# mLSTM head vectors broadcast by DMA through a small DRAM tensor; the first block's output projection computed by token halves, with its norm split the same way

## What is computed

```python
def first_block(x, c, ...):                    # the parts that matter here
    # projections: u, v, q, k, mv, o, gates ga / gb, input and forget gates
    # mLSTM branch, 4 heads of 256: running maximum m_t of the gates, then
    s   = (q @ k.T) * exp(dmat - m_t)          # weights of every (token, source) pair
    den = maximum(abs(sum(s)), exp(-m_t))      # floor of the denominator, per token and head
    h   = (s @ v) / den                        # then normed per head, gated
    x = x + gate1 * (merged @ w_out)           # the first output projection, "out1"
    y = rmsnorm(x, norm2_g) * (1 + scale2) + shift2
    x = x + ... squared_relu(y @ w_ff1) @ w_ff2
```

## Time and profile before

| | |
|---|---|
| median of 3 runs | 3258.81 us (3256.1 to 3259.67) |
| the profiled execution's own time | 3258.92 us |
| its span in the profile | 3257.2 us |
| granted PE clock, mean | 0.994 of full |
| PE busy | 3211.0 us, 99% |
| DVE / ACT / POOL busy | 57% / 16% / 7% |

### The profile page before, as it was taken

How to read it: one execution, slowest core, us unless ns; L and a number is a source line. 1 busy time by engine, 2 the same in 40 slices (tenths; PEclk the granted TensorE clock), 3 DMA queues, 4 the chain that set the end, 5 groups by cost and what they waited for, 6 DMA issues and landing times.

```text
span 3257.2 us, 35901 instructions
## 1 busy us (share of the span) xinstructions
PE 3211.0 (99%) x14194; PEld 2556.8 (78%) x14194; DVE 1849.5 (57%) x3204; ACT 514.0 (16%) x1068; POOL 226.4 (7%) x197
## 2 busy tenths in 40 slices
PE   9999999999999999999899999999999998999999
PEld 3888744888888888884478888888888744788888
DVE  6357835664337764453766664466644537766643
ACT  2111121000001000114521000110001145210001
POOL 1244400000000000003000000000000030000000
PEclk9999999999999999999999999999999999999999
DMA  5244311222222222223012222222222230122221
GB/s 235 91 172 164 117 52 45 72 91 91 88 84 91 82 86 84 97 73 123 1 52 79 90 91 81 88 91 91 84 88 88 73 123 1 53 91 79 90 81 62
DMA packets 43207, 286.16 MB, mean 88 GB/s; under 512 B 5248, under 2 KB 5248, under 8 KB 12064
## 3 DMA queue, kind: packets, MB, share of 16 engines
q1 hardware_dynamic: 39024, 271.14, 23.5%
q0 software_dynamic: 4016, 12.73, 1.2%
HBM read 279.66 MB, written 2.10 MB: 87 GB/s over the span
## 4 chain that ended last, share of the span: by engine, by line
PE 92%; DVE 5%; DVEq 1%; ACT 1%; issue 1%; DMA 0%; ACTq 0%; POOL 0%
PE ps L847 76%; PE ps L555 4%; PE ps L536 3%; PE ps L1226 2%; PE ps L1194 1%; PE ps L874 1%; DVE arena L1820 1%; PE ps L954 1%; DVE arena L2213 1%; ACT arena L1521 1%; PE ps L1208 1%; DVEq L2226 1%; PE ps L1233 0%; PE ps L1165 0%; PE ps L1158 0%
## 5 line engine op out<-in xcount | busy, mean ns | idle before, releaser
L847 PE MATMUL ps<-arena 128*128 128x256 f32 x5456 | 1245.1, 379 | 0.7 <-DVE arena L1911 0.6
L847 PEld LDWEIGHTS ps<-arena 128*128 128x128 f32 x5456 | 1036.3, 190 | 142.8 <-DVE arena L1911 1.6
L847 PE MATMUL ps<-arena,ring 128*128 128x256 f32 x2768 | 646.3, 379 | 0.5 <-ACT arena L1266 0.5
L847 PEld LDWEIGHTS ps<-arena,ring 128*128 128x128 f32 x2768 | 525.6, 190 | 72.5 <-ACT arena L1266 0.9
L847 PE MATMUL ps<-xn,ring 128*128 128x256 f32 x2272 | 520.7, 380 | 5.8 <-DVE arena L1636 2.4
L847 PEld LDWEIGHTS ps<-xn,ring 128*128 128x128 f32 x2272 | 432.3, 190 | 72.4 <-issue 9.6
L1630 DVE TENSOR_TENSOR arena<-arena,ps 128x512 f32<-128x512 f32 x169 | 116.0, 687 | 537.2 <-PE ps L847 508.1
L1606 DVE TENSOR_TENSOR arena<-ring 128x512 f32<-128x512 f32 (+1 forms) x190 | 128.3, 675 | 347.5 <-PE ps L847 347.2
L847 PE MATMUL ps<-xn,arena 128*128 128x256 f32 x1264 | 302.2, 379 | 0.0
L847 PEld LDWEIGHTS ps<-xn,arena 128*128 128x128 f32 x1264 | 240.2, 190 | 32.7
L1433 ACT ACTIVATE arena<-arena 128x512 f32<-128x512 f32 x88 | 55.5, 630 | 883.6 <-DVE arena L2091 883.5
(11 more groups left out here) (312 smaller groups left out, 2359.0 us busy)
## 6 DMA issues: line engine op xcount, KB each, us to landing
ring<-in_w_up_a SPq DMA_DIRECT2D x44, 1024.0 KB, 4.8
ring<-in_w_up_b SPq DMA_DIRECT2D x44, 1024.0 KB, 4.8
ring<-in_w_ff SPq DMA_DIRECT2D x32, 1024.0 KB, 4.8
ring<-in_w_ada SPq DMA_DIRECT2D x24, 1024.0 KB, 4.9
ring<-in_w_down_a SPq DMA_DIRECT2D x16, 1024.0 KB, 4.9
ring<-in_w_down_b SPq DMA_DIRECT2D x16, 1024.0 KB, 4.8
ring<-in_w_in SPq DMA_DIRECT2D x14, 1024.0 KB, 4.9
ring<-in_w_out SPq DMA_DIRECT2D x12, 1024.0 KB, 4.9
```

The source lines that it names most:

```text
L847: mm = nc.tensor.matmul(out_ap, w, operand(product, quads[i]), start=at not in opened, stop=last_chunk and i == len(quads) - 1, skip_group ...
```

## The change

**Head vectors.** The spread matmuls and the eight ACT copies are gone. POOL, before its weight sums of chunk 8, waits for `rows_ready` and writes rows 4 and 5 (4 partitions, 16 KB) to a DRAM tensor `cell_rows`. After its last weight sums and `pair_taken` of pair 24 (the target lies where the operands of the first products were) it issues eight transfers, each of which reads one 2 KB row for all 128 partitions (256 KB written). DVE waits for the four of `neg_m`. ACT waits for the four of `e_mt` and squares them in place, four operations of 512, ahead of its first exponentials.

**Output projection.** `out1` runs over the token halves: first 8 tiles with 256 columns into banks 0 to 3, then 8 tiles with 256 columns into banks 4 to 7. In the first half four tiles are interleaved (k 0 to 5 of all four, then k 6 and 7). A ring slot comes free only in the second half. DVE's and ACT's work on a tile has 256 columns and is done twice.

**Second norm.** Per half, one matmul of `ones` with that half of `ssq` (128 x 256) sums and spreads in one; ACT makes the inverse root with Ln and Exp on 128 x 256 into `rq`; DVE scales by `rq`. The first half's sum is issued after tile 1 of the second half, its scaling and shifts between tiles 3 to 6 of it. The second half's sum is issued after product a of `ff1` pair 0, followed by e of pair 0 and a, e of pair 1, which read the first token half only; then the rest of pair 0 (f c d b g, quad by quad), then the rest of pair 1 (g f c d b). The idle matmuls are gone. The weight sums of `ff1` 1 move from tile 6 to behind the activation sums.

```diff
-SPREADS = [(), (0, 1, 2), (3, 4, 5), (6, 7)]
@@ POOL
                 if n == 8:
                     pool.wait_ge(sem("ws_base"), GROUPS)
+                    pool.wait_ge(sem("rows_ready"), 1)
+                    nc.gpsimd.dma_start(cell_rows, rows[:, 4:6, :]).then_inc(sem("rows_out"), 16)
...
+            pool.wait_ge(sem("rows_out"), 16)
+            pool.wait_ge(sem("pair_taken"), FIRST_PAIRS)
+            for hd in range(HEADS):
+                for which, places in enumerate((neg_m, e_mt)):
+                    row = cell_rows[hd:hd + 1, which, :].to_broadcast([P, S])
+                    nc.gpsimd.dma_start(places[:, hd, :], row).then_inc(sem(f"spread_{which}"), 16)
@@ PE, spread_rows
-                for n in SPREADS[st]:
-                    hd, which = n // 2, n % 2
-                    wait(pe, "spread_read", n - 1)
-
-                    pick = consts[0:HEADS, IDENT, hd:hd + 1].to_broadcast([HEADS, P])
-                    nc.tensor.matmul(ps[:, 4 + which, :], pick, rows[:, 4 + which, :], start=True, stop=True)\
-                        .then_inc(sem("spread"), 1)
@@ PE, after the cell
-            pe_product(pe, "out1", lambda k: merged[:, k, :], 0, lambda k: (sem("merged_ready"), k + 1), None, 6)
-            wait_evacuated(pe, "out1", 5)
-            pe_norm(pe, 0, SQUARES["n2", 0] + DT)
-            pe_busy(5, 4)
+            def out1(half, places):
+
+                for t, k in places:
...
+                        elif t >= BANKS:
+                            pe.wait_ge(sem("out1_read"), DT * half + t - BANKS + 1)
+                    if half == 0 and t < BANKS:
+                        pe.wait_ge(sem("merged_ready"), k + 1)
...
+                    mm = nc.tensor.matmul(out1_bank(half, t), ring[:, slot, unit * UNIT:(unit + 1) * UNIT],
+                                          merged[:, k, side(half)], start=(k == 0), stop=(k == DT - 1))
...
+            def out1_sum(half):
+                pe.wait_ge(sem("out1_read"), DT * (half + 1))
+                pe.wait_ge(sem("sq_added"), SQUARES["n2", 0] + DT * (half + 1))
+                nc.tensor.matmul(norm2_sum(half), ones, ssq[:, side(half)], start=True, stop=True)\
+                    .then_inc(sem("n2_sum"), 1)
+
+            out1(0, [(t, k) for t in range(BANKS) for k in range(6)] + [(t, k) for t in range(BANKS) for k in (6, 7)])
+            out1(0, [(t, k) for t in range(BANKS, DT) for k in range(DT)])
+            out1(1, [(t, k) for t in range(2) for k in range(DT)])
+            out1_sum(0)
+            out1(1, [(t, k) for t in range(2, DT) for k in range(DT)])
...
-            for p in range(FF_HALF):
-                seven("ff1", 0, p, UP_QUADS, ff1_operand, ff1_ready if p == 0 else None,
-                      "aefcdbg" if p == 0 else "aebdgcf", by_quads=p == 0)
+            seven("ff1", 0, 0, UP_QUADS, ff1_operand, ff1_ready, "a", more=True)
+            out1_sum(1)
+            seven("ff1", 0, 0, UP_QUADS, ff1_operand, ff1_ready, "e", opened=(3,), more=True)
+            seven("ff1", 0, 1, UP_QUADS, ff1_operand, ff1_ready, "ae", more=True)
+            pe.wait_ge(sem("n2_read"), 2)
+            for p in range(2):
+                seven("ff1", 0, p, UP_QUADS, ff1_operand, ff1_ready, ("fcdbg", "gfcdb")[p], by_quads=p == 0, opened=(0, 3))
+            for p in range(2, FF_HALF):
+                seven("ff1", 0, p, UP_QUADS, ff1_operand)
@@ ACT
+                    act.wait_ge(sem("spread_1"), 16 * HEADS)
+                    for hd in range(HEADS):
+                        nc.scalar.activation(e_mt[:, hd, :], e_mt[:, hd, :], ACT.Square, scale=EPS**0.5)\
+                            .then_inc(sem("floor_made"), 1)
...
+            def norm2_root(half):
+
+                act.wait_ge(sem("n2_sum"), half + 1)
+                nc.scalar.activation(rq[:, side(half)], norm2_sum(half), ACT.Ln, bias=eps_col, scale=1.0 / D)\
+                    .then_inc(sem("n2_read"), 1)
+                act.drain()
+                nc.scalar.activation(rq[:, side(half)], rq[:, side(half)], ACT.Exp, scale=-0.5).then_inc(sem("n2_root"), 1)
...
             for t in range(DT):
+                out1_square(0, t)
+            for t in range(DT):
+                out1_square(1, t)
+                if t == 1:
+                    norm2_root(0)
+                if 3 <= t < 7:
+                    shifted(0, 2 * t - 6)
+                    shifted(0, 2 * t - 5)
+            norm2_root(1)
+            for n in range(DT):
+                shifted(1, n)
@@ DVE
-            dve.wait_ge(sem("spread_read"), 2 * HEADS)
+            dve.wait_ge(sem("spread_0"), 16 * HEADS)
...
+            for t in range(DT):
+                out1_tile(0, t)
+            for t in range(DT):
+                out1_tile(1, t)
+                if 3 <= t < 7:
+                    dve.wait_ge(sem("n2_root"), 1)
+                    scaled(0, 2 * t - 6)
+                    scaled(0, 2 * t - 5)
+                if t == 5:
+                    next_sums(FIRST_PAIRS)
+            dve.wait_ge(sem("n2_root"), 2)
+            for n in range(DT):
+                scaled(1, n)
                 if n in (3, 5):
                     xn2_sums(n // 2 - 1)
             for q in (2, 3):
                 xn2_sums(q)
+            next_sums(FIRST_PAIRS + 1)
+            dve.wait_ge(sem("n2_sum"), 2)
+            nc.vector.memset(ssq[:, :], 0.0)
```

More of the change, by code:

```diff
@@ L520, in body @@
             def body(it, places):
[L521 to L526, removed]
+                for u in places:
+                    for k in range(K):
                         unit = u * K + k
@@ L541, in body @@
                     if between is not None:
-                        between(it * per + group[-1][0])
+                        between(it * per + u)
             steps(nc.tensor, total, per, body)
@@ L604, in pe_busy, with side, out1_bank, norm2_sum @@
                 nc.tensor.matmul(ps[:, bank, :], ones, consts[:, 0:4, :], start=True, stop=True)
[L606 to L623, removed]
-            dve.wait_ge(sem("nrm_sum"), n + 1)
-            nc.vector.tensor_scalar(nrm[:, 0, :], ps[:, 7, 0:ST], 1.0 / width, EPS, ALU.mult, ALU.add)
-            dve.drain()
-            nc.vector.reciprocal(nrm[:, 1, :], nrm[:, 0, :]).then_inc(sem("nrm_recip"), 1)
-            dve.wait_ge(sem("nrm_root"), n + 1)
-            for st in range(ST):
-                last = nc.vector.tensor_scalar(ssq[:, st * P:(st + 1) * P], ident, nrm[:, 2, st:st + 1], None,
-                                               ALU.mult)
-            last.then_inc(sem("nrm_diag"), 1)
-            dve.wait_ge(sem("nrm_scale"), n + 1)
-            nc.vector.memset(ssq[:, :], 0.0)
-            dve.drain()
+        def side(half):
+            return slice(half * HALF, (half + 1) * HALF)
+        def out1_bank(half, t):
+            return ps[:, BANKS * half + t % BANKS, 0:HALF]
+        def norm2_sum(half):
+            return ps[:, 1 + half, 0:HALF]
+        def wait_out1(eng, half, t):
+            if half and t % 2:
+                slot, before = chunk("out1", t // 2, 0, 0, 0)
+                eng.wait_ge(sem(f"used{slot}"), before + 1)
+            else:
+                eng.wait_ge(sem("out1_tile"), DT + t // 2 + 1 if half else t + 1)
         def act_norm(act, n):
@@ L855, in seven @@
                             mm.then_inc(sem("last_blocks"), 1)
-                        elif (product, i) == places[-1]:
+                        elif (product, i) == places[-1] and not more:
                             mm.then_inc(sem(f"used{slot}"), 1)
@@ L994, in ff1_ready @@
                 if product in "aef":
-                    return sem("xn2"), 2 * quad + (1 if product == "a" else 2)
+                    return sem("xn2"), 2 * quad + {"a": 1, "e": 2, "f": DT + 2}[product]
                 return sem("xn2_sums"), quad + 1
```

79 lines of the change are left out of this document (39 added, 40 removed).

## The result

| | before | changed |
|---|---|---|
| median | 3257.45 us of 4 runs (3254.34 to 3259.67) | 3235.45 us of 4 runs (3234.93 to 3236.0) |
| profiled execution, own time | 3258.92 us | 3236.0 us |
| its span | 3257.2 us | 3234.2 us |

The ratio is 0.9933, 95% interval 0.9921 to 0.9944: 22.0 us less by the medians, 23.0 by the spans, where 21.1 were forecast. The forecast was 3237.8, range 3235 to 3243. It was counted down from the profiled execution's 3258.92, which is 1.5 us above the median of these four runs.

What follows compares the result with a forecast made beforehand. The prediction took PE, holding 92% of the chain that ended last, to bound the kernel. Savings of 12.7 + 8.4 = 21.1 us from the profiled 3258.92 gave 3237.8 us, range 3235 to 3243.

Steps and rivals of the forecast that it cites:

- Part 1: Removing the spreads from PE between the turn of the columns and the second half of `mv`: 12.7 us less.
- No fall behind the turn: PE's clock stays up after the turn of the columns, about 1 us before `mv`; a fall would cost 2.9 us.
- Transfers landed at some 415, needed by 441: Head-vector transfers, issued at 399.3 us, land around 415; landing as late as 441 costs nothing.
- The projection, 0.4 for the columns and 0.4 for the sum: Output projection in 256-column matmuls costs 0.4 us more, and the first half's sum matmul 0.4 more.
- The norm, E + 25.7: From projection end E, `ff1` pair 1 ends 25.7 us later against 34.9 before: 9.2 less.
- Part 2: Projection by token halves and second norm covered by `ff1` products: 8.4 us less, bounds 5.4 to 9.5.
- The nine idle matmuls fall away at no cost, if the clock stays.: Dropping PE's filler matmuls at the second norm costs 0 us, provided the granted clock holds.
- each late us costing one: Norm bound: DVE's chain 3 us later, each late us costing PE one after 0.3 of slack; gain only 5.4.
- The clock falls once more: Rival: PE's clock falls behind the turn of the columns or at projection end, costing 2.9 us: 3240.7; chance 10%.
- DVE bounds the norm: Rival: DVE's 256-column operations keep most of their 512-column duration, chain ends 3 us later: 3240.8; chance 12%.
- Part 1 pays little: Rival: the cell hangs on something other than `mv`, so half of 12.7 us is gained: 3244; chance 4%.
- Transfers one at a time: Rival: POOL's eight transfers go singly, 8.5 us each, landing at 467, making the kernel slower: 3264; chance 3%.

Runs made afterwards that it cites:

- narrow: Changed kernel plus two groups of three dead matmuls of 4 rows x 512 columns, after `mv` tiles 1 and 2: 3242.98 us, ratio 0.996.
- wide: Changed kernel plus two groups of three dead matmuls of 128 rows x 512 columns, after `mv` tiles 1 and 2: 3239.73 us, ratio 0.995.
- part1_only: Kernel before with head vectors by transfers and no spreads, projection and norm as before: 3244.81 us, ratio 0.9966.
- late_a: Changed kernel with the eight transfers issued only after the first tile of the second half of `mv`: 3234.85 us.
- late_b: Changed kernel with the eight transfers issued only after the third tile of the second half of `mv`: 3253.29 us, ratio 0.9992.
- no_cover: Changed kernel with products a and e of `ff1` pair 1 put back behind the waits: 3238.52 us, ratio 0.9949.
- sums_early: Changed kernel with the weight sums of `ff1` 1 put back behind tile 6 of the projection's second half: 3239.74 us, ratio 0.995.
- sums_at_4: Changed kernel with the weight sums of `ff1` 0 moved from tile 5 to tile 4 of the projection's second half: 3234.36 us, ratio 0.9932.
- twos: Kernel before with its eight spreads in four groups of two instead of groups of 3, 3 and 2: 3254.61 us, ratio 0.9995.
- part2_only: Changed kernel with PE's spreads and ACT's copies back, so only projection and norm differ from before: 3245.49 us, ratio 0.9969.
- part2_again: Second run, unchanged, of the changed kernel with PE's spreads and ACT's copies back: 3249.81 us, ratio 0.9972.

## Why the prediction was right

- **Part 1, 12.7 less** (12.1 to 13.0). Between the two profiled executions it was 12.97: the way back to `mv` from the turn cost nothing, where 0.3 were taken. The mechanism, a clock fall behind matmuls of 4 rows, is shown by `narrow` against `wide`. But the size was read from one execution as if it belonged to the code. Some 7.8 us of it belong to the code, 1.6 to 6.8 to the execution: 9.6 to 14.6 in all. The bounds 12.1 and 13.0 were too narrow for that. That the forecast held is in part luck: the execution that was read lost 5.2 us to the clock, the second most of the four profiled, and its whole time is 1.1 to 3.2 us above the medians of the five sets. The reading "the way back may cost up to 0.9", taken from the second group's 3.5 us, was wrong too: the granted clock is 0.63 from 420 to 424, so most of it was the clock, already falling within the group; a group of two without a fall takes 1.91, 0.2 over its own time.
- **No fall behind the turn.** Right for the turn alone: in each of the seven profiled kernels without narrow matmuls behind the turn or idle ones (the changed one, `part1_only`, `late_a`, `late_b`, `no_cover`, `sums_early`, `sums_at_4`) the 48 matmuls of `mv` stand in one row of 41.47 us. The reason given, that 1.9 us of narrow work is harmless, does not hold: in `twos` 1.9 us of spreads behind the turn did lower the clock.
- **Transfers landed at some 415, needed by 441.** They were there at 409.6. Two errors pulled against each other: a transfer took 5.2 us in the median, more than the 1.9 to 4.4 allowed, and they overlapped more than the taken value, the near end of the range. The need of 441 was right by luck of the path. The text derived it from DVE's `cell_args`; `late_b` shows that ACT's queue binds instead, and its 7.36 us put the point at 441.1. POOL's write was issued at 186.65, its weight sums began 0.7 us later than before and ended 1.5 us later (194.3, before 192.8), and nothing waited for them.
- **The projection, 0.4 for the columns and 0.4 for the sum.** Before 54.94 us; now 498.93 to 554.61 = 55.68 with the first sum, against the 55.3 + 0.4 of the text. No wait on banks, no slot late.
- **The norm, E + 25.7** (E is the end of the projection). It was E + 25.28. The wait at the second sum was 0.4 instead of 0.5: DVE was 0.4 late at tile 7, not 0.6. The wait of 0.6 at the third quad was 0.09: a quad's scalings and sums took 0.79 + 1.84 = 2.63 (from 561.88 to 564.51), not 0.85 + 1.95 = 2.8, so DVE's last sums came at E + 14.4, not 15.1. Part 2 is thus 8.87, not 8.4: the term of the DVE chain was too long by 0.7, which took 0.5 off PE's wait.
- **"The nine idle matmuls fall away at no cost, if the clock stays."** It stayed; PE waited 0.4 us only. `sums_early` and `no_cover` show what it hung on: PE waits of 3.0 us, and of 2.2 in two pieces, were followed by a fall there. The bound "each late us costing one" was wrong on that side; a chain of DVE some 3 us later (`sums_early`) costs 5.5 in the profile and 4.3 in the medians, not 3.
- **Rivals.** *The clock falls once more* (10%) did not happen. The granted clock is 1.00 from 499 to 554 and on to 580. The Trainium skill (TensorE: Matmul & The Clock Gate, "A second HAM failure mode: psum-queue depth-cycling") lets the clock swing where PE cycles through banks with short idles. The projection does cycle through banks in 16 groups of eight, but without idles: PE is busy 55.00 of the 55.00 us. So it does not test that rule, and neither do the undisturbed pairs of `ff1` at 12.09 us that the prediction held against it, since 28 matmuls of 0.432 fill them. The single wait of 0.4 us was not followed by a fall; only the longer ones of `no_cover`, `sums_early` and `late_b` were. *DVE bounds the norm* (12%) fell: scaling 0.39 to 0.48, sums 0.42. *Part 1 pays little* (4%) fell with `part1_only`. *Transfers one at a time* (3%) fell: eight in some 10 us, where this rival needed 7.9 each.

Thus 21.1 forecast and 23.0 between the profiled spans: 0.27 from part 1, 0.47 from part 2, 1.16 from outside both, above.

## What to carry to other kernels

Work that uses few of TensorE's rows was paid twice here, 7.8 us in its own time and 1.6 to 6.8 in the clock behind it. If such work only spreads data that are known early, transfers can do it at no cost, as long as they land before the work that is queued behind the wait on them is needed; in `late_b` that was ACT's release of PSUM banks, not the transfer's own reader. Where one engine's result bounds the next product, look for matmuls of other products whose operands are ready: they fill the wait and keep the clock. A price read from one trace belongs to one execution where the clock is in it: look whether the spread of the runs is as wide as the price.

## What the runs showed of the hardware

- The same code got one or two low-clock stretches of different length in different executions. Sets of runs of the kernel before spread over 4.8 to 13.0 us (3251.3 to 3264.3 in the widest), `part2_only`, `part2_again` and `narrow` over 4.7 to 6.8, `twos` over 3.5. Versions without narrow matmuls behind the turn spread over 1.0 (`wide`) to 3.5 us (`sums_at_4`).
- Narrow matmuls are not the only place. Between 355 and 375 us the granted clock is 0.91 in the profiles of before and of the changed kernel and 1.00 in the other twelve; there both profiles lose the same, so their difference is not touched.
- Around waits of PE the clock fell three times: behind one of 2.98 us (0.88 in the stretch of the wait, 0.50 behind it), behind 0.89 and 1.32 us close together, and during one of 16.09 us. A wait of 0.4 us in the changed kernel did nothing.
- Eight transfers of 256 KB, each reading one row of 2 KB for 128 partitions, landed in 5.2 us in the median and all within about 10 us of the first issue, where the slow transfer of 512 KB at the program's start took 8.5. Beside weight loads, at 406 GB/s for both together, it was 7.5.
